# A third merge gate pair by the seven-product scheme, with every product group one ordinary piece sooner and its DRAM sums paced anew

## The reference, cut to what matters

```python
proj = h @ w_in[i]                        # 2048 columns of g_a, 2048 of g_b at its end
merged = jax.nn.sigmoid(g_a) * (y_a @ w_up_a[i]) + jax.nn.sigmoid(g_b) * (y_b @ w_up_b[i])
x = x + merged @ w_o[i]
hid = rmsnorm_2(x, ffn_norm_g[i]) @ w_ffn_in[i]
gate, up = hid[..., :FFN_HIDDEN], hid[..., FFN_HIDDEN:]
x = x + (jax.nn.silu(gate) * up) @ w_ffn_out[i]
```

## Time and profile before

| | before |
|---|---|
| median of 3 runs | 1996.32 us (1995.8 to 1998.2) |
| profiled execution, its own time | 2001.18 us |
| its span (first to last instruction) | 1999.4 us |
| mean granted TensorE clock | 0.998 |
| busy: PE, DVE, ACT, POOL | 1984.3, 1452.0, 1130.5, 109.7 us |

### The profile page before, as it was taken

The page is one execution under the profiler, slowest core; times in us unless marked ns, Lnnn a source line. Parts: engine busy times, 40 slices in busy tenths (PEclk is TensorE's granted clock), DMA queues, the critical chain, the costliest instruction groups (busy, mean ns, idle before and its releaser), DMA issues.

```text
span 1999.4 us, 23507 instructions
## 1 busy us (share of the span) xinstructions
PE 1984.3 (99%) x9150; PEld 1649.0 (82%) x9150; DVE 1452.0 (73%) x1550; ACT 1130.5 (57%) x1402; POOL 109.7 (5%) x132
## 2 busy tenths in 40 slices
PE   9999999999999999999999999999999999999999
PEld 7888888888888878888888888888878887888887
DVE  6878776555666666767777656978888888898765
ACT  7545444554465456556656445666666666666553
POOL 2000000000001110000000000000000000000000
PEclk9999999999999999999999999999999999999999
DMA  9778797999999998766867655787878787887653
GB/s 378 253 246 276 236 329 264 332 316 327 285 303 298 313 333 267 237 226 231 268 220 238 232 183 217 226 300 247 268 240 314 247 263 243 301 255 239 210 182 126
DMA packets 84383, 523.37 MB, mean 262 GB/s; under 512 B 10096, under 2 KB 10864, under 8 KB 38384
## 3 DMA queue, kind: packets, MB, share of 16 engines
q1 hardware_dynamic: 71456, 452.39, 60.1%
q0 software_dynamic: 12672, 69.21, 18.3%
q10 hardware_dynamic: 144, 0.26, 0.0%
HBM read 517.11 MB, written 96.99 MB: 307 GB/s over the span
## 4 chain that ended last, share of the span: by engine, by line
PE 85%; DVE 7%; DMA 6%; ACT 1%; issue 1%; ACTq 0%; DVEq 0%
PE acc L1341 43%; PE acc L1346 21%; PE aux L1698 10%; PE aux L1702 5%; DVE wlo L2506 3%; DMA ple<-in_w_ffn_in 3%; DMA raw<-in_w_ffn_out 2%; DVE wlo L1850 2%; PE aux L1324 1%; PE aux L1414 1%; DMA raw<-in_w_in 1%; DVE ple L2501 1%; ACT whi L1163 1%; ACT whi L914 0%; DMA raw<-in_w_ffn_in 0%
## 5 line engine op out<-in xcount | busy, mean ns | idle before, releaser
L1850 DVE TENSOR_TENSOR wlo<-raw,whi 128x1024 fp32r<-128x1024 f32 x528 | 643.9, 1225 | 407.6 <-ACT whi L914 398.4
L914 ACT ACTIVATE whi<-raw 128x1024 fp32r<-128x1024 f32 x527 | 555.2, 1058 | 610.5 <-PE acc L1346 500.5
L1341 PE MATMUL acc<-whi,actA_hi 128*128 128x512 f32 x892 | 352.7, 395 | 1.2 <-ACT whi L914 1.2
L1341 PE MATMUL acc<-whi,actA_lo 128*128 128x512 f32 x892 | 348.4, 391 | 0.0
L1341 PE MATMUL acc<-whi,actB_hi 128*128 128x512 f32 x860 | 337.6, 393 | 0.2 <-DVE actB_lo L2623 0.2
L1341 PE MATMUL acc<-whi,actB_lo 128*128 128x512 f32 x860 | 334.8, 389 | 0.0
L1163 ACT ACTIVATE whi<-ple 128x1024 fp32r<-128x1024 f32 x176 | 183.9, 1058 | 101.3 <-PE acc L1346 54.5
L1346 PE MATMUL acc<-wlo,actA_hi 128*128 128x512 f32 x892 | 238.8, 389 | 0.0
L2506 DVE TENSOR_TENSOR wlo<-ple,whi 128x1024 fp32r<-128x1024 f32 x176 | 211.3, 1220 | 35.1 <-ACT whi L1163 31.4
L1346 PE MATMUL acc<-wlo,actB_hi 128*128 128x512 f32 x860 | 231.2, 391 | 3.4 <-DVE wlo L1850 3.4
L1341 PEld LDWEIGHTS acc<-whi,actA_hi 128*128 128x128 f32 x892 | 168.0, 188 | 36.2 <-ACT whi L914 1.6
(11 more groups left out here) (350 smaller groups left out, 2312.2 us busy)
## 6 DMA issues: line engine op xcount, KB each, us to landing
raw<-in_w_in SPq DMA_DIRECT2D x116, 1024.0 KB, 7.4
raw<-in_w_ffn_out SPq DMA_DIRECT2D x44, 1024.0 KB, 7.2
summed<-in_w_ffn_in POOLq DMA_DIRECT2D x36, 1024.0 KB, 11.8
raw<-in_w_ffn_in SPq DMA_DIRECT2D x72, 512.0 KB, 6.3
ple<-summed SPq DMA_DIRECT2D x22, 1024.0 KB, 4.8
raw<-summed SPq DMA_DIRECT2D x44, 512.0 KB, 7.2
ple<-in_w_ffn_in SPq DMA_DIRECT2D x18, 1024.0 KB, 7.2
ple<-in_w_ffn_in POOLq DMA_DIRECT2D x36, 512.0 KB, 9.4
```

The lines of the kernel that those rows point to most:

```text
L914: act.activation(whi[:, g % RING], raw_piece(g), ACT.Copy).then_inc(hi_ready, 1)
L1341: pe.matmul(acc2(n)[:, t, :], act[x][:, k + c, t * P:(t + 1) * P], whi[:, g % RING, c, :], start=(p == 0 and c == 0 and x == 0), stop=False)
L1850: dve.tensor_tensor(wlo[:, g % RING], raw_piece(g), whi[:, g % RING].bitcast(F32), ALU.subtract)\
```

## The change

Slab pair 2 of the merge becomes a third seven-product group. The ordinary pieces left in the merge stage are shared out as 10, 10 and 8. In `add_block` the rule that hands out product pieces uses t in place of t - 1, so in all groups, the nine of the feed-forward stage too, each product comes one ordinary piece earlier: M1 x4 after t1, M2 x4 after t2, M7 x4 after t3, M4 x4 after t7, and t8, t9 follow without products between. `FILLS` is not changed. The new group needs four more sums in DRAM. `SUM_AT` has 24 entries up to piece 139 (23 up to 138 before), 7 from 144 to 192 (8 from 144 to 193) and 17 from 199 to 274 (13 from 199 to 271). The remaining edits let the three groups use `gate[0]`, `merge_gate` and `gate[1]` in turn for their results, and take away the ordinary gates of slab pair 2. Piece numbers from the merge stage on shift by up to 12.

```diff
-MERGE_S = [1, 3]
+MERGE_S = [1, 2, 3]
...
-    (1, [("gB", 0), ("uB", 0), ("gA", 2)]),
-    (3, [("uA", 1), ("uB", 1), ("uA", 2), ("gB", 2), ("uB", 2)]),
+    (1, [("gB", 0), ("uB", 0, 0, 0, 2)]),
+    (2, [("uB", 0, 0, 2, 4), ("uA", 1), ("uB", 1)]),
+    (3, [("uA", 2), ("uB", 2)]),
...
-SUM_STEP = 5.2
+SUM_STEP = 5.0
...
         for t, x in enumerate(std):
             self.after[c, t] = self.g
             self.add_std(x, 2)
-            upto = max(0, min(28, (t - 1) * 28 // (len(std) - 3)))
+            upto = max(0, min(28, t * 28 // (len(std) - 3)))
             while done < upto:
                 self.add_s(c, done)
                 done += 1
...
-        SUM_AT = [int(24 + SUM_STEP * i) for i in range(int(116 // SUM_STEP) + 1)] + [144 + 7 * i for i in range(8)]
-        SUM_AT += [199 + 6 * i for i in range(13)]
+        SUM_AT = [int(24 + SUM_STEP * i) for i in range(int(116 // SUM_STEP) + 1)] + [144 + 8 * i for i in range(7)]
+        SUM_AT += [199 + int(4.7 * i) for i in range(17)]
...
-        hid_of = lambda c: merge_h[c] if c < M_GROUPS else (*hid_s, hid_std)[HID_S[c - M_GROUPS]]
+        hid_of = lambda c: MERGE_A[MERGE_S[c]] if c < M_GROUPS else (*hid_s, hid_std)[HID_S[c - M_GROUPS]]
+        second_of = lambda c: MERGE_B[MERGE_S[c]] if c < M_GROUPS else gate[1]
...
-                for role, j in (("gA", 0), ("gB", 0), ("gA", 2), ("gB", 2)):
+                for role, j in (("gA", 0), ("gB", 0)):
```

More of the change, by code:

```diff
@@ L1168, in s_copies @@
                     s_done(act, c, "M1")
+                    if 0 < c < M_GROUPS and MERGE_S[c] == 2:
+                        u_used(act, "uA", 0)
                     act.activation(hid_of(c)[:, 0, :], s_bank(c, "M1"), ACT.Copy).then_inc(sem("s_first"), 1)
@@ L1172, in s_copies @@
                     if 0 < c < M_GROUPS:
-                        u_used(act, "uB", BLOCKS[c - 1][0])
-                    act.activation(gate[1][:, 1, :], aux[:, 1, :], ACT.Copy).then_inc(sem("s_fifth"), 1)
+                        u_used(act, "uB", max(0, MERGE_S[c] - 2))
+                    act.activation(second_of(c)[:, 1, :], aux[:, 1, :], ACT.Copy).then_inc(sem("s_fifth"), 1)
                 if g == S_AT[c, "M6", 3] + 3:
                     act.wait_ge(piece_used, S_AT[c, "M6", 3] + 1)
-                    act.activation(gate[1][:, 0, :], s_bank(c, "M6"), ACT.Copy).then_inc(sem("s_sixth"), 1)
+                    act.activation(second_of(c)[:, 0, :], s_bank(c, "M6"), ACT.Copy).then_inc(sem("s_sixth"), 1)
             def merged_hi(s):
@@ L1214, in _ @@
                         for u in range(T):
-                            ins = act.activation(gate[1][:, u, :], gate[1][:, u, :], ACT.Sigmoid, scale=r_e[:, u:u + 1])
+                            ins = act.activation(second_of(c)[:, u, :], second_of(c)[:, u, :], ACT.Sigmoid, scale=r_e[:, u:u + 1])
                         ins.then_inc(sem("s_gate"), 1)
@@ L2519, in s_gates @@
                 dve.wait_ge(sem("s_sixth"), c + 1)
-                dve.tensor_tensor(hid_of(c)[:, 1, :], gate[1][:, 0, :], aux[:, 2, :], ALU.add).then_inc(sem("s_second_row"), 1)
-                dve.tensor_tensor(gate[1][:, 0, :], aux[:, 1, :], gate[1][:, 0, :], ALU.subtract).then_inc(sem("s_first_row"), 1)
+                dve.tensor_tensor(hid_of(c)[:, 1, :], second_of(c)[:, 0, :], aux[:, 2, :], ALU.add).then_inc(sem("s_second_row"), 1)
+                dve.tensor_tensor(second_of(c)[:, 0, :], aux[:, 1, :], second_of(c)[:, 0, :], ALU.subtract).then_inc(sem("s_first_row"), 1)
                 dve.wait_ge(sem("s_fifth"), c + 1)
                 dve.wait_ge(sem("s_second_row"), c + 1)
-                dve.tensor_tensor(gate[1][:, 1, :], gate[1][:, 1, :], hid_of(c)[:, 1, :], ALU.subtract).then_inc(sem("s_gate_in"), 1)
+                dve.tensor_tensor(second_of(c)[:, 1, :], second_of(c)[:, 1, :], hid_of(c)[:, 1, :], ALU.subtract).then_inc(sem("s_gate_in"), 1)
             def s_merge(c):
```

2 lines of the change are left out of this document (removed).

## The result

| | before | after |
|---|---|---|
| median of the runs | 1996.41 us (1995.8 to 1998.2, 4 runs) | 2006.46 us (2005.07 to 2010.23, 4 runs) |
| profiled execution, time and span | 2001.2, 1999.4 | 2005.07, 2003.3 |

The change made the kernel slower: ratio 1.0047, 95% interval [1.0035, 1.006], 10 us between the medians. The forecast was 2005 us.

A forecast was written before the change was run, and what follows sets the result against it. TensorE, busy 1984.3 of 1999.4 us, was taken to set the end by its matmuls and a few short holes. Terms -5.4 - 5.3 + 9.4 + 1 + 9 = +8.7 us on the 1996.3 median gave 2005 us, range 1993 to 2014.

The forecast's parts named there:

- Part 1: Slab pair 2 of the merge: 168 matmuls in place of 192, 24 fewer on TensorE, -5.4 us.
- Part 2: Borders between feed-forward groups: w_ffn_out loads get 10.9 us instead of 5.4, so holes close, -5.3 us (-3 to -6).
- Part 3: Five d fills at t3 of feed-forward groups stand bare before M7, so TensorE waits: +9.4 us (7 to 12).
- The term for group 7: The fill in feed-forward group 7: a residual addition ahead of the low part makes its wait 2.45 us, not 1.74.
- Part 4: Third merge group: two M7 halves have 4.1 us from issue to need, the first may reach TensorE: +1 us (0 to 3).
- Part 5: Block 2's input: added DRAM sums back up the DMA engines and delay piece 236's load, +9 us (0 to 15).
- this sign of the prediction: Block 2's input: TensorE idle 10 us or more between 655 and 864 us, instead of 3.4.
- the DMA engines take the sums in: Rival on block 2's input: added sums fit, that part 0 to 1 us, sum +0.2, 1996.5 us; chance 0.22.
- The 12 us that the prediction named by that rule: Block 2's input: with queues served in turn, POOL's accumulates halve SP's load rate, the term nearer 12 than 9 us.
- the pacing closes the hole: Rival: piece 236's load lands early enough, block 2's input about -4.5 instead of +9, 1991.5 us; chance 0.13.
- the backlog feeds on itself: Rival: loads after 236 also late, slow restarts; block 2's input 15, merge 3, sum +17, 2013 us; chance 0.15.

The follow-up runs named there:

- rule_fills: Kernel before with products one ordinary piece sooner and the seven d fills one or two ordinary pieces sooner: 1994.26 us, ratio 0.9981.
- rule_undone: Changed kernel with the product-piece rule put back to t - 1: 2012.88 us, ratio 1.0075.
- eighth: Run both, with product pieces of the merge group of 8 ordinary pieces spread over six gaps, not five: 1989.91 us, ratio 0.9954.
- two_between: Run no_burst, with a second ordinary piece between M6's fourth and M4's fourth piece in the third merge group: 1985.14 us, ratio 0.9935.
- pace_alone: Kernel before with only the new pacing of its 44 sums: 2006.04 us, ratio 1.0043.
- sums_late: Changed kernel with the old 13 sums at six pieces in block 2's input, last four sums from w_o on: 1999.49 us, ratio 1.001.
- rule_alone: Kernel before with only the planner line changed, t in place of t - 1: 2003.11 us, ratio 1.0024.
- thin: Run eighth, with 4 sums from piece 199 to the load for 236, one more between 144 and 192, eight behind 241: 1986.1 us.
- both: Changed kernel with d fills moved sooner, old 13 sums at six pieces in block 2's input, last four from w_o on: 1989.59 us, ratio 0.9959.
- no_burst: Run thin, with the four late copies no longer ahead of the loads of resid: 1985.26 us, ratio 0.9941.

## Why the prediction was right

The forecast was right in time (2005 for 2006.46) and its sum of +8.7 stands against +10.05 between the medians. That the two come within 1.5 us is in part luck: against the traces the fills and the sums were put too high and the borders and the merge hole were sized too low, and the medians differ by more than the profiled executions do (below). By its steps:

- **Part 1** (-5.4): busy TensorE fell by 5.6 us, matmuls by 24. Right.
- **Part 2** (-5.3): the border holes were 6.4 us and are gone in every kernel with the rule; w_ffn_out is waited for no more. Right in mechanism. As a saving of time it is less certain than the holes: rule_fills ran only 3.5 us under before, with 1.6 us of a new hole. What I left out is the merge stage: its three groups have borders as well, and the rule also saved about 9 us of holes there that the third group would have opened (`rule_undone`). The forecast was not harmed, as I had put no border cost on that stage.
- **Part 3** (+9.4): four of 1.70 and one of 1680.55 - 1678.36 - 0.36 = 1.83 make 8.6 (7.7 as holes, which are counted from the last of the four transposes and not from the first); moving the fills gave 8.9 us on the kernel before and 7.7 in the full change. The mechanism was right at all five places, and 9.4 was 0.8 too much. The term for group 7 was too large (2.45 taken): the addition to the residual there ran beside ScalarE's high copy and held the low part up for 0.1 us.
- **Part 4** (+1): the size was 1.9 and the step that failed is the named place. The M7 halves were not late: ScalarE's waits for summed fell to 5.0 us. It was M4's accumulate by POOL, which I had not costed. In after, the fourth accumulates of all groups land 8.3 to 10.6 us after their issue, this one at the upper end. In the group of 8 pieces the four pieces by which the splits run ahead are all short there, where a group of 10 has an ordinary one among them; spreading the pieces brought 1.9 us of lead (`eighth`); a whole ordinary piece more ended the wait (`two_between`).
- **Part 5** (+9): 8.3 alone, 7.0 when taken out. The load for piece 236 landed 7.3 us later than before; I had said near 730, it was 725.8. TensorE lacks 8.55 us in that window and not 10 or more, so this sign of the prediction failed narrowly. With the matmuls at half clock (below), which count as busy, the holes are 11.7 us, 6.4 more than before; 9 was too much by that trace, and near what the medians of pace_alone and sums_late say.

Of the rivals, "the DMA engines take the sums in" rested on a rate: 359 GB/s wanted, 356 seen. From 620 to 760 us neither after nor pace_alone reached it: after moved 320 to 330 GB/s at a share of 0.98, as a sum holds the engines longer for each MB than a load does (5.3 us for the accumulate alone against 2.7, by the prediction's reading of the earlier trace rows). With plain loads alone the kernel before moves far more, here on SP's queue:

```profile
20.00:40.00 20.00, 20.00 (x90) 16.53 (x90) 13.63 (x20) 14.29 (x28) 0.00 (x0) 1.00 1.02 421
```

The Trainium skill, DMA: Bandwidth & Descriptors, "Specifications", gives about 358 GB/s as the limit of a core's HBM traffic. The 421 GB/s of this row go past it, and the measurement decides: here that figure was neither a limit nor a measure of what fits. The share of the engines' time was: 0.95 before, 0.98 after, and no room for 16 us more.

The Trainium skill, DMA: Bandwidth & Descriptors, "Queues, rings and completion order", says that each DMA engine serves the queues with work in turn. The load for piece 236 took 29.0 us for 22.9, which agrees with it, but a longer backlog in any order would do the same, and no run tells the two apart. The 12 us that the prediction named by that rule were not seen; 8.3 and 7.0 were nearer the term I took.

The other two rivals fell as well. The one in which the pacing closes the hole wanted ScalarE's wait under 3 us; it was 13.95. The one in which the backlog feeds on itself wanted late loads and holes further on; behind 752 us block 2's input has the same 0.9 us of holes in both traces.

In the profiled executions the sum nearly closes: input stage +6.4, borders -6.4, fills +7.7, merge +1.9, matmuls -5.4, a spell at half clock near 296 us that only the profile of before has -1.7, together +2.5 against +3.9 of span; gaps under 0.33 us are not in it. The medians have more: the rule with the fills moved -3.5, the bare fills +8.9, the pacing +8.3 and the third pair -4.4 make +9.3 of the +10.05.

What stays open: why an accumulate takes 8.3 us in one group and 13.7 in another run's third merge group was only argued (loads beside it), and no run took the three loads away. And what the medians of rule_alone, pace_alone and after have beyond the holes of their traces was not found.

## What to carry to other kernels

When a reordering wins lead for loads, look at every fixed table that was laid out against the old order. Here one line was a loss of 5.4 us and, with seven entries of a table moved with it, a gain of 3.5. Background copies are to be paced by the busy share of the DMA engines in the stretch where they stand, not by a rate in GB/s, and kept away from a burst: around one 2 MB store two sums more cost 7 to 8 us and three fewer gave 3.8 (the distance from the burst was not tested by itself). The merge of the third pair was sound: with both mended the full change runs in 1989.6 us, 0.41% under before, and with fewer sums ahead of piece 236 and a longer lead for the accumulate (`two_between`) in 1985.1, 0.65% under.

## What the runs showed of the hardware

Behind some of the long holes TensorE ran at half clock for a while. After the 4.52 us wait at 728.74 in the kernel after, nine matmuls start 0.43 us apart and then again 0.23; the window below has the granted clock at 0.72 (2.4 GHz in part, 1.2 in the other). A hole of 4.7 us so cost 2.2 more. The length of the wait alone does not tell whether this follows: behind a wait of 1.87 us that ended at 1739.5 in rule_undone the matmuls became slow, behind one of 3.29 us that ended at 752.3 in pace_alone they did not.

```profile
728.00:740.00 12.00, 11.26 (x41) 9.43 (x42) 5.08 (x8) 9.69 (x8) 0.00 (x0) 0.72 1.02 339
```

```profile
731.34 0.63 PE L1343 MATMUL acc<-whi,actB_hi 128*128 128x512 f32 x1
731.76 0.63 PE L1343 MATMUL acc<-whi,actB_lo 128*128 128x512 f32 x1
...
735.48 0.39 PE L1343 MATMUL acc<-whi,actB_lo 128*128 128x512 f32 x1
735.71 0.39 PE L1343 MATMUL acc<-whi,actB_hi 128*128 128x512 f32 x1
```

More surprising is a spell of it without an idle TensorE: in some executions (seven of the thirteen profiles, before and thin among them), not in others (after and both among them), the granted clock is 0.83 or 0.84 from 290 to 300 us with TensorE busy for all of it, at a cost of 1.7 us. Here is `thin`:

```profile
290.00:300.00 10.00, 10.00 (x40) 7.67 (x40) 7.24 (x14) 2.87 (x4) 0.00 (x0) 0.83 1.06 377
```

What TensorE did before it are twelve small matmuls, which use 4 rows of input. In before the last eight of them start at 293.60, and the matmuls of 512 columns that follow start 0.43 us apart. In after the same twelve stand from 293.75 on, and the next ones start 0.23 us apart. So they don't bring the spell in every execution.

```profile
293.60 1.97 PE L1473 MATMUL aux<-hrow,sel 4*128 4x256 f32 x8
...
296.41 0.63 PE L1341 MATMUL acc<-whi,actA_hi 128*128 128x512 f32 x1
296.84 0.63 PE L1341 MATMUL acc<-whi,actA_lo 128*128 128x512 f32 x1
```

An accumulating DMA of 512 KB from DRAM into SBUF, the fourth of its group, landed 8.3 to 10.6 us after its issue in after and 13.7 in no_burst; the first of a group took as little as 6.4. Plain loads of twice the size took about 5 us where the engines were free. So a buffer that is accumulated into beside other loads is to be planned with up to 14 us of lead, not with that of a load.
